# Rearranging the start of a two-block transformer kernel: two load queues, rounding by k-tile, the second unit in halves, the third split moved

## The reference, cut to what matters

```
def _rms(x, g):
    y = x * lax.rsqrt(jnp.mean(x * x, axis=-1, keepdims=True) + EPS)
    return y * g

rq, rk, rv, rg, gq, gf, gi, gg = _split_cols(_rms(x, mix_norm_g[0]) @ ev_w_in[0], EV_SIZES)
rq = _rotary(_split_heads(rq, RET_HEADS), pos)      # 512 columns: the first two jobs
rk = _rotary(_split_heads(rk, RET_HEADS), pos) * (RET_DK ** -0.5)
```

## Time and profile before

| what | value |
|---|---|
| median of 3 runs | 3120.41 us (3119.22 to 3122.66) |
| span of the profiled execution, first to last instruction | 3119.4 us |
| TensorE matmuls busy | 3097.3 us, 99% |
| VectorE busy | 1563.7 us, 50% |
| ScalarE busy | 1063.2 us, 34% |
| mean granted TensorE clock | 0.997 |

### The profile page before, as it was taken

One profiled execution on the slowest core, in us unless ns is written; L12 is line 12 of the kernel. 1 busy time (PEld: TensorE's weight loads), 2 busy tenths in 40 slices (PEclk: granted clock), 3 DMA queues, 4 the chain that ended last, 5 costly groups with the idle time before them and its releaser, 6 DMA issues.

```text
span 3119.4 us, 37101 instructions
## 1 busy us (share of the span) xinstructions
PE 3097.3 (99%) x15540; PEld 2594.3 (83%) x15540; DVE 1563.7 (50%) x1889; ACT 1063.2 (34%) x1155; POOL 237.6 (8%) x139
## 2 busy tenths in 40 slices
PE   9999999999999999999999999999999999999999
PEld 7798988888889798888888778888888878888887
DVE  7564555554335554555435764544433766444432
ACT  3223343443223433444323332333323332333321
POOL 0002100010000020010000000111000000100100
PEclk9999999999999999999999999999999999999999
DMA  4412412223321131222233122222232322222222
GB/s 170 115 55 73 144 55 90 99 94 108 120 97 68 48 142 55 85 99 99 95 108 116 58 92 101 90 99 93 103 108 89 95 82 95 95 95 96 94 106 95
DMA packets 47567, 297.72 MB, mean 95 GB/s; under 512 B 7075, under 2 KB 7331, under 8 KB 13396
## 3 DMA queue, kind: packets, MB, share of 16 engines
q1 hardware_dynamic: 42336, 285.91, 25.9%
q10 hardware_dynamic: 5108, 10.02, 1.4%
HBM read 291.16 MB, written 4.75 MB: 95 GB/s over the span
## 4 chain that ended last, share of the span: by engine, by line
PE 91%; DVE 5%; ACT 2%; issue 1%; DMA 0%; ACTq 0%; POOL 0%; DVEq 0%; SPq 0%
PE G L460 83%; DVE wL L1688 1%; ACT wH L1255 1%; PE psS L816 1%; DVE mxt L1920 1%; PE psS L520 1%; PE psS L1017 1%; PE psS L1134 0%; PE G L1143 0%; PE G L1024 0%; PE psT L552 0%; DVE ws L2477 0%; PE psT L1170 0%; PE G L1058 0%; PE psS L949 0%
## 5 line engine op out<-in xcount | busy, mean ns | idle before, releaser
L460 PE MATMUL G<-hH,wH 128*128 128x512 f32 x2560 | 1015.4, 397 | 9.1 <-DVE wL L1688 3.9
L460 PE MATMUL G<-hH,wL 128*128 128x512 f32 x2560 | 998.8, 390 | 0.0
L460 PE MATMUL G<-hL,wH 128*128 128x512 f32 x2560 | 997.7, 390 | 0.0
L1688 DVE TENSOR_TENSOR wL<-raw,wH 128x2048 fp32r<-128x2048 f32 x260 | 626.5, 2410 | 634.3 <-ACT wH L1255 634.0
L460 PE MATMUL G<-wsr,wH 128*128 128x512 f32 (+1 forms) x2512 | 745.9, 380 | 0.4
L1255 ACT ACTIVATE wH<-raw 128x2048 fp32r<-128x2048 f32 x263 | 501.7, 1908 | 591.7 <-PE G L460 573.1
L460 PEld LDWEIGHTS G<-hH,wH 128*128 128x128 f32 x2560 | 481.5, 188 | 124.1 <-issue 20.3
L460 PEld LDWEIGHTS G<-hH,wL 128*128 128x128 f32 x2560 | 481.0, 188 | 102.3
L460 PEld LDWEIGHTS G<-hL,wH 128*128 128x128 f32 x2560 | 481.9, 188 | 97.9 <-issue 1.2
L460 PEld LDWEIGHTS G<-wsr,wH 128*128 128x128 f32 x2512 | 464.3, 189 | 91.0 <-issue 1.5
L460 PE MATMUL G<-wsr,wL 128*128 128x512 f32 (+1 forms) x1256 | 476.1, 379 | 0.0
(11 more groups left out here) (291 smaller groups left out, 2510.3 us busy)
## 6 DMA issues: line engine op xcount, KB each, us to landing
raw<-in_units SPq DMA_DIRECT2D x263, 1024.0 KB, 4.8
ws<-bias_rows SPq DMA_DIRECT2D x2, 1536.0 KB, 14.7
bias_rows<-ws ACTq DMA_DIRECT2D x1, 2560.0 KB
x<-in_x SPq DMA_DIRECT2D x4, 512.0 KB, 7.5
ws<-in_mem ACTq DMA_DIRECT2D x2, 1024.0 KB, 4.7
ws<-bias_rows ACTq DMA_DIRECT2D x1, 2048.0 KB, 8.2
out_x<-x SPq DMA_DIRECT2D x3, 512.0 KB, 7.1
ws<-in_decay ACTq DMA_DIRECT2D x1, 1280.0 KB, 7.6
```

Of the source, the lines that this page charges most:

```text
L460: mm = pe.matmul(o, mv if swap else wt, wt if swap else mv, start=first and n == 0, stop=last and n == 2)
L1688: V.tensor_tensor(wL[:, g.p, :], raw[:, g.p, :], wH[:, g.p, :].bitcast(F32), ALU.subtract)\
```

## The change

- Loads: SyncE issues k-tiles 0 and 1 of x as two transfers of 256 KB and no longer the first half of unit 0. ScalarE's queue issues that half, as two quarters, before its first other work.
- Job 0: unit 0's first half is rounded, split and handed over in quarters (two k-tiles each), by turns with the k-tiles of x. The squares of x are put behind later k-tiles.
- Job 1: unit 1 is rounded and split in halves. TensorE begins job 1 with the first half and takes the second at k-tile 4. Function `start_jobs` takes the place of `first_jobs` here: `total` moves from k-tile 7 of job 0 to k-tile 3 of job 1, and `spread` from k-tile 2 to k-tile 5 of job 1. On VectorE, the tails of unit 1 stand between the second and the third `fold`.
- Job 2: VectorE splits unit 2 right after the root mean square, ahead of the rotary table and of the read-out of job 0. ScalarE's order for it stays (after job 0), and its four table loads stay ahead of it, now behind both halves of unit 1.
- TensorE does 14 instead of 16 matmuls on constants.

```diff
@@ -342,6 +342,7 @@
         kv_ready, keys_ready = sem("kv_ready"), sem("keys_ready")
         out_done, tile_done, tile_out = sem("out_done"), sem("tile_done"), sem("tile_out")
         pair_ready, last_ready = sem("pair_ready"), sem("last_ready")
+        first_in, second_in = sem("first_in"), sem("second_in")
         g_in, half_in, w0_round, w0_ready, rot_in = (sem("g_in"), sem("half_in"), sem("w0_round"), sem("w0_ready"),
                                                      sem("rot_in"))
         b_done, b_read = sem("b_done"), sem("b_read")
@@ -394,8 +395,8 @@
                 sp.dma_start(x[:, 2 * m:2 * m + 2, :], a["x"][:, 2 * m:2 * m + 2, :]).then_inc(x_in[m], 16)
 
             sp.dma_start(par1[:], a["par1"]).then_inc(g_in, 16)
-            load_x(0)
-            sp.dma_start(raw[:, 0, 0:half], a["units"][0][:, 0:half]).then_inc(half_in, 16)
+            sp.dma_start(x[:, 0, :], a["x"][:, 0, :]).then_inc(x_in[0], 16)
+            sp.dma_start(x[:, 1, :], a["x"][:, 1, :]).then_inc(second_in, 16)
             load_x(1)
             sp.dma_start(raw[:, 0, half:UNIT], a["units"][0][:, half:UNIT]).then_inc(raw_in[0], 16)
             load_x(2)
@@ -596,13 +597,11 @@
                     if mem and jj == 1:
                         spread(w=M)
 
-            def first_jobs(spread_out=True, halves_in=False):
+            def first_jobs(spread_out=True):
 
 
                 def first(k):
 
-                    if halves_in and k == 4:
-                        take_unit()
                     pe.wait_ge(rl_ready, c.rw.v + k + 1)
                     if k == KT - 1:
                         total()
@@ -611,15 +610,38 @@
                     if k == 2 and spread_out:
                         spread()
 
-                if halves_in:
-                    pe.wait_ge(w0_ready, 1)
-                    take_job()
-                    end_job(two_tiles(h_op, range(KT), operand=first))
-                    c.unit.off += 1
-                else:
-                    plain(h_op, operand=first)
+                plain(h_op, operand=first)
                 c.rw.off += 8
                 plain(h_op, operand=second)
+
+            def start_jobs():
+
+                def first(k):
+
+                    if k in (0, 2):
+                        pe.wait_ge(w0_ready, k // 2 + 1)
+                    elif k == 4:
+                        take_unit()
+                    pe.wait_ge(rl_ready, c.rw.v + k + 1)
+
+                def second(k):
+
+                    if k == 3:
+                        total()
+                    elif k == 4:
+                        take_unit()
+                    elif k == 5:
+                        spread()
+
+                take_job()
+                end_job(two_tiles(h_op, range(KT), operand=first))
+                c.unit.off += 1
+                c.rw.off += 8
+
+                pe.wait_ge(w0_ready, 3)
+                take_job()
+                end_job(two_tiles(h_op, range(KT), operand=second))
+                c.unit.off += 1
 
             def attention(rows, nk, probs, score, pv, per_job, scores_read, l, keys_read, fill):
 
@@ -694,7 +716,7 @@
 
 
             pe.wait_ge(consts, 5)
-            for n in range(16):
+            for n in range(14):
                 pe.matmul(psT[:, 1, 0:P], ident[:], ones[:], start=True, stop=True)
 
             def bias_rows(part):
@@ -716,7 +738,7 @@
                 if l == 0:
                     for j in range(6):
                         if j == 0:
-                            first_jobs(halves_in=True)
+                            start_jobs()
                         elif j in (4, 5):
                             token_major(h_op)
                         elif j > 1:
@@ -1388,33 +1410,51 @@
 
             half = UNIT // 2
 
-            def chunk(m):
-
-                act.wait_ge(x_in[m], 16)
-                for k in (2 * m, 2 * m + 1):
+            def tiles(ks):
+
+                for k in ks:
                     activation(hH[:, k, :], x[:, k, :], ACT.Identity, scale=col1(0, "mix", k)).then_inc(rh_ready, 1)
                     c.rw.off += 1
 
+            def rounded(u, w0, w1, done):
+
+                activation(wH[:, u, w0:w1], raw[:, u, w0:w1], ACT.Copy).then_inc(done, 1)
+
+            quarter = UNIT // 4
+            for n, arrived in enumerate((half_in, first_in)):
+                act.dma_start(raw[:, 0, n * quarter:n * quarter + quarter],
+                              a["units"][0][:, n * quarter:n * quarter + quarter]).then_inc(arrived, 16)
             act.wait_ge(consts, 5)
             activation(rden[:, 0:1], neghalf[:], ACT.Identity)
             act.wait_ge(g_in, 16)
-            chunk(0)
+            act.wait_ge(x_in[0], 16)
+            tiles((0,))
             act.wait_ge(half_in, 16)
-            activation(wH[:, 0, 0:half], raw[:, 0, 0:half], ACT.Copy).then_inc(w0_round, 1)
+            rounded(0, 0, quarter, w0_round)
+            act.wait_ge(second_in, 16)
+            tiles((1,))
+            act.wait_ge(first_in, 16)
+            rounded(0, quarter, half, w0_round)
+            act.wait_ge(x_in[1], 16)
+            tiles((2, 3))
+            act.wait_ge(raw_in[0], 16)
+            rounded(0, half, UNIT, wh_ready)
+            act.wait_ge(x_in[2], 16)
+            tiles((4, 5))
             square(x[:, 0:2, :])
-            chunk(1)
             square(x[:, 2:4, :])
-            act.wait_ge(raw_in[0], 16)
-            activation(wH[:, 0, half:UNIT], raw[:, 0, half:UNIT], ACT.Copy).then_inc(wh_ready, 1)
-            c.unit.off += 1
-            for m in (2, 3):
-                chunk(m)
-                square(x[:, 2 * m:2 * m + 2, :])
+            act.wait_ge(x_in[3], 16)
+            tiles((6, 7))
+            square(x[:, 4:6, :])
+            act.wait_ge(raw_in[1], 16)
+            rounded(1, 0, half, w0_round)
+            rounded(1, half, UNIT, wh_ready)
+            c.unit.off += 2
+            square(x[:, 6:8, :])
             act.dma_start(ws[:, ROT:ROT + 2, :], a["rotary"].rearrange("p (a b) -> p a b", b=S)).then_inc(rot_in, 16)
             act.dma_start(rb33[0:32, :], a["rel_bias"]).then_inc(b33_in, 16)
             act.dma_start(oh33, a["onehot"].rearrange("k (b w) -> k b w", b=3)).then_inc(b33_in, 16)
             act.dma_start(ws[:, DEC:DEC + 5, :], a["decay"].rearrange("p (a b) -> p a b", b=S)).then_inc(table_in, 16)
-            split()
 
             def bias_exps():
                 act.wait_ge(bias_sub, 1)
@@ -2015,35 +2055,50 @@
 
             half = UNIT // 2
 
-            def low(m):
-
-                dve.wait_ge(x_in[m], 16)
-                for k in (2 * m, 2 * m + 1):
+            def low(ks):
+
+                for k in ks:
                     dve.wait_ge(rh_ready, c.rw.v + 1)
                     V.scalar_tensor_tensor(hL[:, k, :], x[:, k, :], col1(0, "mix", k), hH[:, k, :].bitcast(F32),
                                            ALU.mult, ALU.subtract).then_inc(rl_ready, 1)
                     c.rw.off += 1
 
+            def tail(u, w0, w1, done):
+
+                V.tensor_tensor(wL[:, u, w0:w1], raw[:, u, w0:w1], wH[:, u, w0:w1].bitcast(F32), ALU.subtract)\
+                    .then_inc(done, 1)
+
+            quarter = UNIT // 4
             dve.wait_ge(g_in, 16)
-            low(0)
+            dve.wait_ge(x_in[0], 16)
+            low((0,))
             dve.wait_ge(w0_round, 1)
-            V.tensor_tensor(wL[:, 0, 0:half], raw[:, 0, 0:half], wH[:, 0, 0:half].bitcast(F32), ALU.subtract)\
-                .then_inc(w0_ready, 1)
-            low(1)
+            tail(0, 0, quarter, w0_ready)
+            dve.wait_ge(second_in, 16)
+            low((1,))
+            dve.wait_ge(w0_round, 2)
+            tail(0, quarter, half, w0_ready)
+            dve.wait_ge(x_in[1], 16)
+            low((2, 3))
+            dve.wait_ge(wh_ready, 1)
+            tail(0, half, UNIT, wl_ready)
+            dve.wait_ge(x_in[2], 16)
+            low((4, 5))
             fold(1)
-            dve.wait_ge(wh_ready, 1)
-            V.tensor_tensor(wL[:, 0, half:UNIT], raw[:, 0, half:UNIT], wH[:, 0, half:UNIT].bitcast(F32), ALU.subtract)\
-                .then_inc(wl_ready, 1)
-            c.unit.off += 1
-            low(2)
+            dve.wait_ge(x_in[3], 16)
+            low((6, 7))
             fold(2)
-            low(3)
+            dve.wait_ge(w0_round, 3)
+            tail(1, 0, half, w0_ready)
+            dve.wait_ge(wh_ready, 2)
+            tail(1, half, UNIT, wl_ready)
+            c.unit.off += 2
             fold(3)
-            split()
             dve.wait_ge(consts, 5)
             rstd(4, ST, D)
             columns(0)
             by_token(1)
+            split()
 
             dve.wait_ge(rot_in, 16)
             dve.wait_ge(rb_ready, c.bc.v)
@@ -2088,7 +2143,7 @@
                     for j in range(6):
                         if j < 4:
                             o = (QR, KR)[j // 2] + 2 * (j % 2)
-                            step(rotary(ws[:, o:o + 2, :]))
```

(1 more changed line is left out.)

## The result

| kernel | median of 20 runs | lowest to highest |
|---|---|---|
| before | 3120.42 us | 3118.57 to 3122.85 |
| changed | 3127.97 us | 3123.20 to 3133.00 |

The changed kernel is slower: ratio 1.0021, 95% interval 1.0015 to 1.0027. I had forecast 3119.3 in 3116.6 to 3122.4. Its runs also lie further apart, 10 us against 4: six at 3123.2 to 3124.6 with a mean granted clock of 0.997, fourteen at 3125.7 to 3133.0 with 0.994 to 0.996. The runs list that a time is 1.8 us longer than its span. By that the profiled execution of the kernel before lies at about 3121.2 (an estimate), above its median, and the 1.0 us that I took was the distance between two executions. The forecast is the same without it: 3120.4 - 1.06.

A forecast was written before the change was run, and what follows sets the result against it. TensorE's matmuls, 99% of the span, bound the kernel. Job 2 at 34.15 instead of 35.21 gains 1.06 us: 3119.4 - 1.06 = 3118.3 for the span, with 1.0 to the median 3119.3, range 3116.6 to 3122.4.

The forecast's parts named there:

- the 4.7 us that could be gained at most: TensorE's waits up to job 2: upper bound on the gain, 0.15% of the time, below the 0.2% that a measurement tells.
- What it gains, the end gains: Start of job 2 taken as the measure: its gain, 1.06 us, was to reach the end of the kernel.
- one stretch at the lower clock: Later in the program: TensorE's moved waits might add or remove one stretch at 1.2 GHz, 1.7 us.
- k-tile 0 at 6.5: First loads: the first k-tile of x usable at 6.5 us, so that job 0 starts at 8.75.
- my 1,250: First loads: thousands of bytes moved by 7.0 us in the model of arrivals, at 200, then 250 GB/s.
- behind both quarters: First loads: k-tile 0 waits for both quarters of unit 0's half, 913 thousand bytes, there at 6.6 us.
- Fewer constants cost nothing: Start, before job 0: 14 instead of 16 constants cost nothing, since they end two us ahead of TensorE's start.
- VectorE's path to the free bank: Jobs 1 and 2: root mean square, split, table and read-out free job 0's bank at 34.1; job 2 starts at 34.15.
- The new wait: Before job 2: TensorE stands 1.5 us for job 0's bank, where before it stood 0.54 us for unit 2's split.
- (a): Rival, chance 0.27: second queue speeds first loads; 2.8 us gained, 3117.6; sign: rates above 300 GB/s before 7 us.
- (b): Rival, chance 0.20: VectorE's queue reaches the root mean square too late; from 0.4 us gained to 1.8 lost.
- (c): Rival, counted in (b)'s chance: early split of unit 2 only swaps places with the read-out; whole change loses 1.7 us, 3122.1.

The follow-up runs named there:

- e1: The changed kernel with 24 instead of 14 matmuls on constants at the start: 3123.07 us, ratio 1.0010 to the kernel before.
- e4: The kernel before with 6 instead of 16 matmuls on constants: 3124.04 us, ratio 1.0007 to the kernel before.
- e3: The kernel before with the changed kernel's loads alone, order of work and 16 constants as before: 3124.52 us, ratio 1.0012.
- e2: The changed kernel with the loads of the kernel before, all issued by SyncE, and 14 constants: 3121.87 us, ratio 1.0002.
- e5: The changed kernel as it is, measured again on another chip: 3125.97 us, ratio 1.0015 to the kernel before.
- e8: The changed kernel with all first loads on SyncE, in order of use: 3123.22 us, ratio 1.0004 to the kernel before.
- e12: The changed kernel with the contents of SyncE's and ScalarE's load queues exchanged: 3121.80 us, ratio 1.0003 to the kernel before.
- e7: The changed kernel with four matmuls on constants added between job 1 and job 2: 3124.55 us, ratio 1.0010 to the kernel before.
- e11: The changed kernel, its own loads, with 24 constants at the start and four before job 2: 3122.80 us, ratio 1.0008.
- e6: The changed kernel with the loads of before, 17 constants at the start and four before job 2: 3120.01 us, ratio 0.9999.
- e10: The same kernel as e6 with more runs: 3120.95 us, ratio 0.9999 to the kernel before.

## Why the prediction was wrong, step by step

- **What bounds the kernel, and the 4.7 us that could be gained at most.** Right as a bound on the gain. I drew from it that the change hardly matters and did not ask the same of a loss. "What it gains, the end gains" holds up to the mark: job 2 and the mark are both 3.2 us late. It does not hold for a single execution's end, where the work behind the mark differs by up to 4.4 us from trace to trace, more than the 1.7 us that I allowed for one stretch at the lower clock.
- **Loads: k-tile 0 at 6.5.** This step failed first. It was taken up at 8.1 to 8.6 in the traces of the changed kernel and of e1. The total rate was not what failed: 138 and 329 GB/s make 1,332 thousand bytes by 7.0, more than my 1,250. The order was: I took "behind both quarters", 913 thousand bytes, as the latest place, and by these rates they had passed at about 5.7, 2.4 us before the k-tile was taken up. The sum put job 0 at 8.75; it came at 10.45, 1.7 us later.
- **"Fewer constants cost nothing."** This step failed with it. The constants end at 7.07, and 3.4 us of standing followed where I had reckoned two. I had seen 2.48 us pass at a granted clock of 1.00 and named no rival in which the clock falls at the start. Job 0 was to last 11.15 us and lasted 13.70, 2.55 more, by matmuls at the slower pace. e4 makes the same fall with data and order of before; e1, with the clock kept at the start, has less than half of the loss. Whether two more constants would have been enough isn't shown: e3, with 16, stood 4.7 us and its clock fell too.
- **Job 1 and job 2: VectorE's path to the free bank.** Right to a tenth: job 2 was to start 14.25 us after job 1, and did so after 14.29. The new wait was 1.8 us (I had 1.5). So the 4.29 us between my 34.15 and the measured 38.44 are the two steps above, 1.70 and 2.55, and 0.04 here. With the old loads (e2) job 0 at 8.73 and job 2 at 33.99 are my 8.75 and 34.15, by loads that happen to feed it at the same time.
- **What a new stop costs.** I priced the wait for the bank by its length. It has a second price: in e1, e5, e8 and e12 the matmuls behind it ran at the lower clock, in the traces of the changed kernel and of e2 they did not. Bridging it took 1.4 us from the median (e5 to e7) and 1.5 us at the mark (248.92 and 247.40).
- **The rivals.** (a) is refuted for this arrangement: its sign appeared, 329 GB/s before 7 us, but the k-tile that job 0 needs came later. (b) had the sign, but its mechanism did not decide: job 1 was late because job 0 was, not because of VectorE. (c), the early split being no gain by itself, wasn't tried alone.

Together, at the mark: the changed loads cost 1.8 us by lateness (e11 against e6; job 0 starts at 10.42 and 8.66), and the stops' lower clock 2.8 in the changed kernel's trace, which has the first fall alone, and 3.35 in e5's, which has both (against e11). The other changes gain 1.3 (e6, with its bridges). The medians say the same more coarsely: the changed kernel stands 4.9 to 7.6 us above before (e5, first measurement), 2.3 without both falls (e11), and with the old loads as well between -1.0 and 0.4 (e6, e10). What stays open: of the 7.6, the trace shows 3.2 at the mark, in the fastest run; the slower ones list a lower granted clock, but where in the program it fell isn't traced. Why the first measurement lies 2 us above e5, and why the same stop is followed by the lower clock in one execution and not in the next, stays open too.

## What to carry to other kernels

Where TensorE fills 99% of the time, look for what makes it stand, and price a stop twice: by its length and by the clock that can fall behind it. A few matmuls on constants, put where it would stand anyway, did not delay what followed (job 2 at 33.97 with the bridge, 33.99 without) and in all four traces with a bridged second stop (e6, e7, e10, e11) the clock stayed up behind it. When two operands are needed together, check in the trace when each lands: here a second queue brought one of them earlier and the other later, while one queue in order of use brought both early and the pieces behind them late. And compare positions at a mark close behind the change as well as medians, since the end carries what happens later.
